# Feed-forward up products with channels as rows: high and low activations move together, wide products before narrow ones

## The chip, the cores and the metric

The kernel runs on one core of one Trainium2 chip. The metric is the device time of one execution, in microseconds (us), the median of several runs.

## What is computed

Two transformer blocks on 256 tokens of width 2048, one after the other, all in float32. The change lies in the last stage, the feed-forward part of the second block. It projects the normalised tokens to 2 x 5632 channels, convolves each channel causally over three tokens, multiplies one half with the silu of the other and projects back:

```
D_MODEL = 2048
FFN_HIDDEN = 5632
CONV_WIDTH = 3
...
def causal_dwconv(u, w, bias):
    ch = u.shape[-1]
    y = lax.conv_general_dilated(u, w[:, None, :].astype(u.dtype), window_strides=(1,),
                                 padding=[(CONV_WIDTH - 1, 0)],
                                 dimension_numbers=('NWC', 'WIO', 'NWC'),
                                 feature_group_count=ch)
    return y + bias
```

In words: `u = rms_norm(x) * (1 + scale) + shift` times `w_up`, `causal_dwconv(u)`, split in two, product with silu, times `w_down`, times a gate, added to `x`.

## The kernel before

**Numbers in two parts.** TensorE works on fp32r operands. To keep float32 accuracy each operand is split into a rounded high part and the low rest. A product is the sum of three: high x high, high x low and low x high. Weights arrive in tiles of two row blocks (`SL = 2`) by 512 channels, 128 x 1024 elements, 512 KB. SyncE loads them into `raw` (8 buffers). ScalarE casts a tile to `hi` (the helper `split`, L728) and VectorE subtracts to get `lo` (L1371), each with 4 buffers (`SPL = 4`); so both run up to four tiles ahead of TensorE and wait for `tile_used`. The activations are already split, in `xh` and `xl`, channel blocks of 128 rows by 256 tokens.

**Token-major products.** `tile` (L2455 to L2457) keeps 128 tokens of the activations in the array and moves 512 weight columns: for each of 2 row blocks and 2 halves of the tokens three products of 512 columns, 12 to a tile. The result has tokens in the rows. Elsewhere in the program `channel_tile` (L2550 to L2552) does it the other way: 128 weight columns stay in the array and 256 tokens move, 24 products of 256 columns to a tile, and the result has channels in the rows.

**The feed-forward stage** goes over `FB = 11` blocks of 512 + 512 channels. For a block, `up_block` takes 16 weight tiles (8 for each half), `down` takes 8 (`c` = 0 to 3, two tiles each). TensorE's order is up(0), up(1), down(0), up(2), down(1) and so on, so that the convolution of a block has a whole up block of time. `half` 0 of the up products is summed in PSUM banks 0 and 1, half 1 in banks 2 and 3, as down uses them in turn as well.

**Between up and down.** ScalarE copies the sum out of PSUM to `UP`, scaled by the root of the norm of each token (`up_evac`, L1274, two instructions of 128x512 to a half). Since the convolution is over tokens, they have to lie along the row: TensorE transposes `UP` to PSUM banks 4 to 7 (`up_turn`, L3132, 8 transposes to a half, 16 to a block). ScalarE then writes the middle tap and the bias to `cv` (`conv_base`, L1283), VectorE adds the other two taps from PSUM (`conv`, L2333, 16 instructions), and silu (L1289), product (L2348), high part `Fh` (L1296) and low part `Fl` (`flow`, L2354) follow. VectorE adds each down result to `Y` (`y_add`, L2377).

**At the stage's head** a row with the norm's square root is put in PSUM bank 7 (`row_of`), VectorE adds shift times that row to the raw activations (`shifted`, L1968 and L1974), ScalarE casts to `xh` (L772, L775), VectorE subtracts to `xl` (`turn_low`). The first up tiles wait for these pair by pair (`turn_lo`).

Of the kernel before, what the change touches and what calls it, by code (L numbers as in the profile page):

```python
# [17 lines left out]
P = 128  # L18
# [3 lines left out]
SL = 2  # L22
# [132 lines left out]
def build(nc, A, out):  # L155
    V, SC, PE_, GP = nc.vector, nc.scalar, nc.tensor, nc.gpsimd
    ctx = ExitStack()
    with ctx:
# [12 lines left out]
        xh = at("xh", [P, KD, S], 64, F32R)  # L171
        xl = at("xl", [P, KD, S], 80, F32R)
# [10 lines left out]
        def C(name, i, n=1):  # L183
# [133 lines left out]
        UP = at("UP", [P, 2, TT, CH], W0 + 32)  # L317
# [79 lines left out]
        up_out, up_T, cv_base, cv_ok, sil_ok, f32_ok, fh_ok, fl_ok, dn_out = (  # L397
            sem(n) for n in ("up_out", "up_T", "cv_base", "cv_ok", "sil_ok", "f32_ok", "fh_ok",
# [136 lines left out]
        def _(pool):  # L535
# [173 lines left out]
            inverse_root(ROOT4, 2, root=True)  # L709
# [8 lines left out]
        def _(act):  # L718
# [49 lines left out]
            def high(n, r):  # L768
                if r == 0:
                    for k in range(2):  # L770
                        act.wait_ge(h_sum, 9 * n + k + 1)
                        SC.copy(xh[:, k], T32[:, k]).then_inc(h_high, 1)  # L772
                    return
# [495 lines left out]
            def up_evac(b, half, n):  # L1269
                act.wait_ge(tile_used, n)  # L1270
                if half == 0 and (not isinstance(b, int) or b):
                    act.wait_ge(up_T, b * 2)
                for t in range(TT):
                    SC.activation(UP[:, half, t], ps[:, 2 * half + t], ACT.Copy,  # L1274
                                  scale=stat[:, ROOT4 + 2 + t:ROOT4 + 3 + t]).then_inc(up_out, 1)

            def conv_base(b, half):

                act.wait_ge(cc_ok, b + 1)
                act.wait_ge(up_T, b * 2 + (half + 1))  # L1280
                for f in range(4):
                    q = 16 * half + 4 * f
                    SC.activation(cv[:, half, f], ps[:, 4 + 2 * half + f // 2, S * (f % 2):S * (f % 2) + S],  # L1283
                                  ACT.Identity, scale=ccol[:, q + 2:q + 3], bias=ccol[:, q + 3:q + 4]
# [71 lines left out]
        def _(dve):  # L1356
# [955 lines left out]
            shifted("h4", 1, 0, 2, ps[:, 7, 0:S])  # L2312
            turn_low(1, 0)
            shifted("h4", 1, 1, 2, ps[:, 7, 0:S])
            shifted("h4", 1, 2, 2, ps[:, 7, 0:S])
            turn_low(1, 1)
            split(BASE["ffn"] + SPL - 1)
            shifted("h4", 1, 3, 2, ps[:, 7, 0:S])
            turn_low(1, 2)

            def conv(b, half):

                for tap in range(2):
# [4 lines left out]
                    for f in range(4):  # L2328
                        q = 16 * half + 4 * f
                        d = 1 + tap  # L2330
                        src = ps[:, 4 + 2 * half + f // 2, S * (f % 2):S * (f % 2) + S - d]
# [39 lines left out]
            def y_add(b, c, n):  # L2371
# [3 lines left out]
                for t in range(TT):  # L2375
                    ys = Y[:, t, c * CH:(c + 1) * CH]
                    V.tensor_tensor(ys, ys, ps[:, 2 * (c % 2) + t], ALU.add).then_inc(dn_out, 1)  # L2377

            def hidden(b, rest):
                conv_cols(b)  # L2380
                rest(2)
                conv(b, 0)
# [5 lines left out]
                flow(b)  # L2388
# [5 lines left out]

            for j in range(2 * TC):
                if j < 4:
                    shifted("h4", 1, 4 + j, 2, ps[:, 7, 0:S])
                split(n0 + SPL + j)
                if j < 5:
                    turn_low(1, 3 + j)  # L2400
            dve.wait_ge(y_zero, 1)
            with dve.Fori(1, FB - 1) as b:
# [4 lines left out]
                hidden(b - 1, rest)  # L2407
                rest(8)
                for c in range(4):
# [4 lines left out]
            hidden(FB - 2, rest)  # L2414
            for c in range(4):
                rest(2)
                y_ready(c)

            conv_cols(FB - 1)
            rest(2)  # L2420
# [17 lines left out]
        def _(pe):  # L2438
# [667 lines left out]
            pe.wait_ge(inv_ok, 2)  # L3106
            row_of(INV, 7)
            keep_busy(9, 6)
            n0 = BASE["ffn"]

            def up_block(b, n, off=0):
                for half in range(2):
                    if not isinstance(b, int):
                        pe.wait_ge(dn_out, b * 8 + (2 * half - 10))
                    elif b:
                        pe.wait_ge(up_out, b * 4 + (2 * half - 2))
                    for j in range(TC):
# [193 lines left out]
```

## Time and profile before

| | |
|---|---|
| median of 3 runs | 3598.34 us (3597.11 to 3598.89) |
| profiled execution, its own time | 3599.18 us |
| span of its profile | 3597.6 us |
| TensorE busy | 3580.8 us |
| VectorE busy | 2667.9 us |
| ScalarE busy | 1782.5 us |
| mean granted TensorE clock | 0.999 of full speed |

The span is the time from the first to the last instruction on the core. An engine's busy time is the sum of the stretches in which it had an instruction under way. A matmul's row in the trace gives a start that can be trusted and an end that is modelled, since products overlap in the array; what a product takes from its neighbours is read from the distance between starts.

### The profile page before, as it was taken

What the parts mean: (1) busy time and instruction counts of PE and PEld (TensorE: products, weight loads), DVE (VectorE), ACT (ScalarE), POOL (GpSimd) and SP (SyncE); (2) the same over time, 40 slices, a digit from 0 to 9 for tenths busy, and PEclk for the clock granted to TensorE, in tenths of its full rate; (3) what the DMA queues carried; (4) which work ended last, traced back from release to release, by engine and by line L of the source; (5) the groups of instructions that cost most, each with busy time, mean ns of one, the idle gap of its engine ahead of it and who ended that gap; (6) DMA issues with size and microseconds to landing.
All of it is one profiled execution on the core that took longest, in us unless ns stands there. A gap on an engine that the chain in (4) does not pass through costs nothing.

```text
span 3597.6 us, 49685 instructions
## 1 busy us (share of the span) xinstructions
PE 3580.8 (100%) x17251; PEld 2993.6 (83%) x17251; DVE 2667.9 (74%) x3480; ACT 1782.5 (50%) x2161; POOL 148.6 (4%) x214
## 2 busy tenths in 40 slices
PE   9999999999999999999999999999999999999999
PEld 7898888888888888888888888878888888888887
DVE  5664567668997877777788887899986656666567
ACT  5554444444444444444444445556754555555444
POOL 4000000000000000000000000010000000000000
PEclk9999999999999999999999999999999999999999
DMA  7546658766668989888887886655556565655654
GB/s 256 170 158 201 193 180 279 270 198 223 206 221 308 356 295 336 298 335 294 339 289 279 279 280 220 184 180 168 168 174 219 174 197 186 192 186 186 192 184 144
DMA packets 211070, 826.96 MB, mean 230 GB/s; under 512 B 24016, under 2 KB 25296, under 8 KB 197088
## 3 DMA queue, kind: packets, MB, share of 16 engines
q1 hardware_dynamic: 177904, 640.23, 53.3%
q10 hardware_dynamic: 15264, 102.99, 7.5%
q0 software_dynamic: 17744, 81.59, 6.2%
q8 instruction: 104, 1.70, 0.2%
q14 instruction: 54, 0.44, 0.0%
HBM read 786.43 MB, written 38.29 MB: 229 GB/s over the span
## 4 chain that ended last, share of the span: by engine, by line
PE 95%; DVE 3%; DMA 1%; issue 1%; ACT 0%; POOL 0%; SPq 0%; ACTq 0%; POOLq 0%; DVEq 0%
PE ps L2455 29%; PE ps L2457 28%; PE ps L2456 28%; PE ps L2811 2%; PE ps L2550 1%; PE ps L2551 1%; PE ps L2552 1%; DVE lo L1371 1%; PE ps L2844 1%; PE ps L2565 1%; PE ps L3132 1%; PE ps L2498 0%; PE ps L2979 0%; DMA act_scratch<-Ab 0%; DVE eq L1773 0%
## 5 line engine op out<-in xcount | busy, mean ns | idle before, releaser
L1371 DVE TENSOR_TENSOR lo<-raw,hi 128x1024 fp32r<-128x1024 f32 x1216 | 1478.4, 1220 | 860.7 <-ACT hi L728 856.9
L728 ACT CAST hi<-raw 128x1024 fp32r<-128x1024 f32 x1216 | 1272.9, 1048 | 1691.4 <-PE ps L2457 1651.2
L2455 PE MATMUL ps<-hi,xh 128*128 128x512 f32 x2880 | 1138.5, 395 | 1.5 <-DVE lo L1371 0.9
L2457 PE MATMUL ps<-hi,xl 128*128 128x512 f32 x2880 | 1123.8, 390 | 0.0
L2456 PE MATMUL ps<-lo,xh 128*128 128x512 f32 x2880 | 1123.2, 390 | 0.0
L2455 PEld LDWEIGHTS ps<-hi,xh 128*128 128x128 f32 x2880 | 541.7, 188 | 117.3 <-issue 6.3
L2457 PEld LDWEIGHTS ps<-hi,xl 128*128 128x128 f32 x2880 | 541.2, 188 | 113.9
L2456 PEld LDWEIGHTS ps<-lo,xh 128*128 128x128 f32 x2880 | 541.9, 188 | 108.7
L2455 PE MATMUL ps<-hi,Ph 128*128 128x512 f32 x1020 | 401.5, 394 | 0.0
L2457 PE MATMUL ps<-hi,Pl 128*128 128x512 f32 x1020 | 397.8, 390 | 0.0
L2456 PE MATMUL ps<-lo,Ph 128*128 128x512 f32 x1020 | 397.3, 390 | 0.0
L2457 PEld LDWEIGHTS ps<-hi,Pl 128*128 128x128 f32 x1020 | 191.5, 188 | 40.2
L2456 PEld LDWEIGHTS ps<-lo,Ph 128*128 128x128 f32 x1020 | 191.8, 188 | 38.5
L2455 PEld LDWEIGHTS ps<-hi,Ph 128*128 128x128 f32 x1020 | 191.6, 188 | 38.5 <-DVE X L1854 0.3
L1854 DVE TENSOR_TENSOR X<-X,ps 128x512 f32<-128x512 f32 x240 | 153.5, 681 | 0.0
L1827 DVE SCALAR_TENSOR_TENSOR macc<-mraw,stat,macc 128x2048 f32<-128x2048 f32 x60 | 140.8, 2346 | 0.2 <-DMA mraw<-in_w_mod 0.2
L2455 PE MATMUL ps<-hi,Fh 128*128 128x512 f32 x348 | 137.7, 396 | 0.7 <-DVE Fl L2354 0.7
L2457 PE MATMUL ps<-hi,Fl 128*128 128x512 f32 x348 | 135.8, 390 | 0.0
L2456 PE MATMUL ps<-lo,Fh 128*128 128x512 f32 x348 | 135.6, 390 | 0.0
L2333 DVE SCALAR_TENSOR_TENSOR cv<-ps,ccol,cv 128x255 f32<-128x255 f32 (+1 forms) x176 | 72.7, 476 | 7.7 <-ACT cv L1283 6.9
L2455 PEld LDWEIGHTS ps<-hi,Fh 128*128 128x128 f32 x348 | 65.4, 188 | 14.4 <-DVE Fl L2354 1.1
L2457 PEld LDWEIGHTS ps<-hi,Fl 128*128 128x128 f32 x348 | 65.3, 188 | 13.8
(478 smaller groups left out, 3574.1 us busy)
## 6 DMA issues: line engine op xcount, KB each, us to landing
raw<-in_peer_u SPq DMA_DIRECT2D x256, 512.0 KB, 4.6
raw<-in_peer_v SPq DMA_DIRECT2D x256, 512.0 KB, 4.6
mraw<-in_w_mod ACTq DMA_DIRECT2D x96, 1024.0 KB, 6.8
raw<-in_w_up SPq DMA_DIRECT2D x176, 512.0 KB, 3.5
raw<-in_w_in SPq DMA_DIRECT2D x143, 512.0 KB, 3.8
raw<-in_in SPq DMA_DIRECT2D x128, 512.0 KB, 3.5
raw<-in_w_down SPq DMA_DIRECT2D x88, 512.0 KB, 4.2
raw<-in_out SPq DMA_DIRECT2D x64, 512.0 KB, 4.2
```

Source lines behind the costliest of these rows:

```text
L728: SC.copy(hi[:, n0 % SPL, 0:w], raw[:, n0 % RAW, 0:w]).then_inc(hi_ready, 1)
L1371: V.tensor_tensor(lo[:, n0 % SPL, 0:w], raw[:, n0 % RAW, 0:w], hi[:, n0 % SPL, 0:w].bitcast(F32), ALU.subtract).then_inc(lo_ready, 1)
L1827: V.scalar_tensor_tensor(macc[:], mraw[:, u % 4], stat[:, 64 + u:65 + u], macc[:], ALU.mult, ALU.add).then_inc(mod_used, 1)
L1854: V.tensor_tensor(xs, xs, ps[:, 4 + 2 * (c % 2) + t], ALU.add).then_inc(v_out, 1)
L2333: ins = V.scalar_tensor_tensor(dst, src, ccol[:, q + 1 - tap:q + 2 - tap], dst, ALU.mult, ALU.add)
L2455: PE_.matmul(acc, xhi[:, k0 + k, xs], H, start=s0, stop=False)
L2456: PE_.matmul(acc, xhi[:, k0 + k, xs], L, start=False, stop=False)
L2457: mm = PE_.matmul(acc, xlo[:, k0 + k, xs], H, start=False, stop=s1)
L2550: PE_.matmul(acc, H, xhi[:, k0 + k], start=first and k == 0 and f % 2 == 0, stop=False)
L2551: PE_.matmul(acc, H, xlo[:, k0 + k], start=False, stop=False)
L2552: mm = PE_.matmul(acc, L, xhi[:, k0 + k], start=False, stop=last and k == SL - 1 and f % 2 == 1)
L2811: mm = PE_.matmul(ps[:, 4 + b, k * P:(k + 1) * P], oh1[:, b, k], oh2[:, b, k], start=True, stop=True)
```

## The change

Up products are made with channels in the rows. The high and low activations become one tensor `xx`, and the high weights meet both in one product whose moving operand is 2 x 256 columns, the high tokens and behind them the low ones; it fills a whole PSUM bank (columns 0 to 255 high x high, 256 to 511 high x low). The low weights meet the high tokens in a product of 256 columns, added to columns 0 to 255. In `up_tile` all 8 wide products of a tile come first and then its 8 narrow ones. An up half takes 4 banks, so the two halves and the four down results each use all 8. ScalarE copies the first half of each bank to `UP` (one instruction), VectorE adds the second half (`up_sum`, new), and the convolution reads `UP`. The transposes are gone, and so is the scaling on the way out: the root is multiplied into the activations ahead of their split (`rooted`, `rooted_low`), and ScalarE adds the shift as it casts.

```
--- before.py
+++ after.py
...
-        xh = at("xh", [P, KD, S], 64, F32R)
-        xl = at("xl", [P, KD, S], 80, F32R)
+        xx = at("xx", [P, 2, KD, S], 64, F32R)
+        xh, xl = xx[:, 0], xx[:, 1]
...
-        UP = at("UP", [P, 2, TT, CH], W0 + 32)
+        UP = at("UP", [P, 2, 4, S], W0 + 32)
...
-            inverse_root(ROOT4, 2, root=True)
+            inverse_root(ROOT4, 2)
...
+                if n == 1:
+                    for k in range(2):
+                        act.wait_ge(h_sum, 9 + (k + 1 if r == 0 else r + 2))
+                        SC.activation(xh[:, 2 * r + k], T32[:, 2 * r + k], ACT.Identity,
+                                      bias=mcol[:, 2, 2 * r + k:2 * r + k + 1]).then_inc(h_high, 1)
+                    return
...
             def up_evac(b, half, n):
                 act.wait_ge(tile_used, n)
-                if half == 0 and (not isinstance(b, int) or b):
-                    act.wait_ge(up_T, b * 2)
-                for t in range(TT):
-                    SC.activation(UP[:, half, t], ps[:, 2 * half + t], ACT.Copy,
-                                  scale=stat[:, ROOT4 + 2 + t:ROOT4 + 3 + t]).then_inc(up_out, 1)
+                if not isinstance(b, int) or b:
+                    act.wait_ge(cv_ok, b * 2 + (half - 1))
+                SC.copy(UP[:, half], ps[:, 4 * half:4 * half + 4, 0:S]).then_inc(up_high, 1)
 
             def conv_base(b, half):
 
                 act.wait_ge(cc_ok, b + 1)
-                act.wait_ge(up_T, b * 2 + (half + 1))
+                act.wait_ge(up_out, b * 2 + (half + 1))
                 for f in range(4):
                     q = 16 * half + 4 * f
-                    SC.activation(cv[:, half, f], ps[:, 4 + 2 * half + f // 2, S * (f % 2):S * (f % 2) + S],
-                                  ACT.Identity, scale=ccol[:, q + 2:q + 3], bias=ccol[:, q + 3:q + 4]
+                    SC.activation(cv[:, half, f], UP[:, half, f], ACT.Identity, scale=ccol[:, q + 2:q + 3], bias=ccol[:, q + 3:q + 4]
                                   ).then_inc(cv_base, 1)
 
...
+            def rooted(r):
+                dve.wait_ge(turn_hi, 2 * (TBASE["h4"] + r) + 2)
+                if r == 0:
+                    for k in range(2):
+                        V.tensor_tensor(T32[:, k], T32[:, k], row4, ALU.mult).then_inc(h_sum, 1)
+                    return
+                both = T32[:, 2 * r:2 * r + 2]
+                V.tensor_tensor(both, both, row4.unsqueeze(1).to_broadcast([P, 2, S]), ALU.mult).then_inc(h_sum, 1)
+
+            def rooted_low(r):
+                for k in range(2):
+                    c = 2 * r + k
+                    dve.wait_ge(h_high, 9 + c + 1)
+                    dve.wait_ge(h_sum, 9 + (k + 1 if r == 0 else r + 2))
+                    low = V.scalar_tensor_tensor(xl[:, c], T32[:, c], mcol[:, 2, c:c + 1], xh[:, c].bitcast(F32),
+                                                 ALU.add, ALU.subtract)
+                    if k:
+                        low.then_inc(turn_lo, 1)
+                    elif r == 0:
+                        low.then_inc(pair_low, 1)
+
+            rooted(0)
+            rooted_low(0)
+            rooted(1)
+            rooted(2)
+            rooted_low(1)
             split(BASE["ffn"] + SPL - 1)
-            shifted("h4", 1, 3, 2, ps[:, 7, 0:S])
-            turn_low(1, 2)
+            rooted(3)
+            rooted_low(2)
 
...
-                        src = ps[:, 4 + 2 * half + f // 2, S * (f % 2):S * (f % 2) + S - d]
+                        src = UP[:, half, f, 0:S - d]
...
+                dve.wait_ge(up_out, b * 2 + 2)
...
-                flow(b)
...
+            def up_sum(b, half, n):
+                dve.wait_ge(tile_used, n)
+                dve.wait_ge(up_high, b * 2 + (half + 1))
+                V.tensor_tensor(UP[:, half], ps[:, 4 * half:4 * half + 4, S:2 * S], UP[:, half], ALU.add).then_inc(up_out, 1)
+
...
                 hidden(b - 1, rest)
+                up_sum(b, 0, off + (n0 + 24))
+                flow(b - 1)
                 rest(8)
+                up_sum(b, 1, off + (n0 + 32))
...
-            pe.wait_ge(inv_ok, 2)
-            row_of(INV, 7)
+            pe.wait_ge(rstd_ready, ROOTS)
+            row_of(ROOT4 + 2, 7)
             keep_busy(9, 6)
             n0 = BASE["ffn"]
+
+            def up_tile(n0, off, k0, bank, first, last, ready=None):
+
+                pe.wait_ge(lo_ready, n0 + 1 + FIRST + off)
+                for k in range(SL):
+                    if ready is not None:
+                        ready(k)
+                    for f in range(4):
+                        H = hi[:, n0 % SPL, k * CH + f * P:k * CH + (f + 1) * P]
+                        both = ps[:, bank + f].rearrange("p (a t) -> p a t", a=2)
+                        PE_.matmul(both, H, xx[:, :, k0 + k], start=first and k == 0, stop=False)
+                for k in range(SL):
+                    for f in range(4):
+                        L = lo[:, n0 % SPL, k * CH + f * P:k * CH + (f + 1) * P]
+                        mm = PE_.matmul(ps[:, bank + f, 0:S], L, xh[:, k0 + k], start=False, stop=last and k == SL - 1)
+                mm.then_inc(tile_used, 1)
 
             def up_block(b, n, off=0):
                 for half in range(2):
                     if not isinstance(b, int):
-                        pe.wait_ge(dn_out, b * 8 + (2 * half - 10))
+                        pe.wait_ge(dn_out, b * 8 + (4 * half - 12))
                     elif b:
-                        pe.wait_ge(up_out, b * 4 + (2 * half - 2))
+                        pe.wait_ge(up_out, half + 1)
                     for j in range(TC):
                         first = isinstance(b, int) and b + half == 0
                         if first and j:
                             pe.wait_ge(turn_lo, TBASE["h4"] + j + 1)
-                        tile(n + TC * half + j, off, xh, xl, SL * j, 2 * half, j == 0, j == TC - 1,
-                             ready=h4_pair if first and j == 0 else None)
-                        if isinstance(b, int) and b < 2 and b + half == 1 and j == 2:
-                            up_turn(0, b)
-
-            def up_turn(b, half):
-                pe.wait_ge(up_out, b * 4 + (2 * half + 2))
-                if not isinstance(b, int) or b:
-                    pe.wait_ge(cv_ok, b * 2 + (half - 1))
-                for f in range(4):
-                    for t in range(TT):
-                        mm = PE_.transpose(ps[:, 4 + 2 * half + f // 2, (f % 2) * S + t * P:(f % 2) * S + (t + 1) * P],
-                                           UP[:, half, t, f * P:(f + 1) * P], ident)
-                mm.then_inc(up_T, 1)
+                        up_tile(n + TC * half + j, off, SL * j, 4 * half, j == 0, j == TC - 1,
+                                ready=h4_pair if first and j == 0 else None)
 
             def down(b, c, n, off=0):
 
@@ -3139,23 +3183,17 @@
...
                     pe.wait_ge(fl_ok, b + 1)
-                elif c >= 2 and sum_open:
-                    pe.wait_ge(cv_ok, 2 * (FB - 1) + c - 1)
-                elif c >= 2 and not last:
-                    pe.wait_ge(dn_out, b * 8 + (2 * c - 2))
-                bank = 2 * c if sum_open or last else 2 * (c % 2)
+                if c % 2 == 0 and not last:
+                    pe.wait_ge(up_out, b * 2 + (3 + c // 2))
...
+            def downs(b, n, off=0):
+
+                for c in range(4):
                     down(b, c, n, off)
```

On TensorE at the head of the loop over blocks, where the down products of block b - 2 begin (`up_out`, `cv_ok`, `fl_ok` are semaphores counted by ScalarE and VectorE, `ISA` and `REGISTER_ALU` rows are waits and the counting of them), before:

```order
L3129 ISA [waits up_out]
L3132 MATMUL ps<-const,UP 128x128 [waits cv_ok]
L3132 MATMUL ps<-const,UP 128x128 x7
L2442 ISA [waits fl_ok]
L2455 MATMUL ps<-hi,Fh 128x512 [waits lo_ready]
```

and after, with the first up tile of the same loop under it:

```order
L3187 ISA [waits fl_ok]
L2482 ISA [waits up_out]
L2495 MATMUL ps<-hi,Fh 128x512 [waits lo_ready]
...
L3153 REGISTER_ALU [waits dn_out]
L3160 MATMUL ps<-xx,hi 128x512 [waits lo_ready]
L3160 MATMUL ps<-xx,hi 128x512 x7
L3164 MATMUL ps<-xx,lo 128x256 x8
```

The transposes have gone from the front of the down products, which now wait for VectorE's sum (`up_out`); an up tile is 8 wide and 8 narrow products where it was 12 wide ones.

On VectorE, behind the product of the convolved halves in the same loop, before:

```order
L2348 TENSOR_TENSOR F32t<-cv,sil 128x1024 [waits cv_ok]
L1369 REGISTER_ALU
L1371 TENSOR_TENSOR lo<-raw,hi 128x1024 [waits hi_ready]
L1369 REGISTER_ALU
L1371 TENSOR_TENSOR lo<-raw,hi 128x1024 [waits hi_ready]
L2354 TENSOR_TENSOR Fl<-F32t,Fh 128x1024 [waits f32_ok,fh_ok]
```

and after:

```order
L2374 TENSOR_TENSOR F32t<-cv,sil 128x1024 [waits cv_ok,sil_ok]
L1372 REGISTER_ALU
L1374 TENSOR_TENSOR lo<-raw,hi 128x1024 [waits hi_ready]
L1372 REGISTER_ALU
L1374 TENSOR_TENSOR lo<-raw,hi 128x1024 [waits hi_ready]
L2423 ISA [waits tile_used]
L2424 TENSOR_TENSOR UP<-ps,UP 128x1024 [waits up_high]
L2380 TENSOR_TENSOR Fl<-F32t,Fh 128x1024 [waits f32_ok,fh_ok]
```

The new sum stands ahead of `Fl`, so `Fl` and the weight splits behind it come after a wait for the last product of an up half (`tile_used`) and for ScalarE's copy (`up_high`). The second sum of a block stands eight splits later.

## Rows read from the trace of the kernel before

**Rows 1.** The page: busy times, the granted clock, the chain by engine.
```profile
PE 3580.8 (100%) x17251; PEld 2993.6 (83%) x17251; DVE 2667.9 (74%) x3480; ACT 1782.5 (50%) x2161; POOL 148.6 (4%) x214
...
PEclk9999999999999999999999999999999999999999
...
PE 95%; DVE 3%; DMA 1%; issue 1%; ACT 0%; POOL 0%; SPq 0%; ACTq 0%; POOLq 0%; DVEq 0%
```

**Rows 2.** Windows: one feed-forward block each; engines' busy us (instructions), clock, DMA.
```profile
3144.20:3211.30 67.10, 67.10 (x306) 55.74 (x305) 42.63 (x51) 35.26 (x41) 0.00 (x0) 1.00 0.58 187
3211.30:3278.40 67.10, 67.10 (x306) 55.74 (x305) 42.62 (x51) 35.25 (x41) 0.00 (x0) 1.00 0.57 188
```

**Rows 3.** Chain that ended last, 3130 to 3290 us: start, us, what.
```profile
3144.16 0.87 PE ps L3132 x8
3150.50 0.87 PE ps L3132 x8
...
3211.26 0.87 PE ps L3132 x8
```

**Rows 4.** Timeline of TensorE, up tiles (24 products between the first and the last row).
```profile
3204.97 0.39 PE L2455 MATMUL ps<-hi,xh 128*128 128x512 f32 x1
3205.20 0.39 PE L2456 MATMUL ps<-lo,xh 128*128 128x512 f32 x1
...
3210.41 0.39 PE L2455 MATMUL ps<-hi,xh 128*128 128x512 f32 x1
```

**Rows 5.** Timeline of TensorE in channel_tile (42 products between first and last row).
```profile
2285.04 0.28 PE L2550 MATMUL ps<-xh,hi 128*128 128x256 f32 x1
2285.16 0.28 PE L2551 MATMUL ps<-xl,hi 128*128 128x256 f32 x1
...
2290.08 0.28 PE L2550 MATMUL ps<-xh,hi 128*128 128x256 f32 x1
```

**Rows 6.** One line's instructions, channel_tile's low weights: ns min/median/max, first and last start.
```profile
L2552 PEld LDWEIGHTS ps<-yh,lo x64: 188/192/193, 2675.6 to 2698.5; 128*128 128x128 f32 x64
```

**Rows 7.** Groups by form, 2900 us to the end: busy us, mean ns, idle before.
```profile
L1371 DVE TENSOR_TENSOR lo<-raw,hi 128x1024 fp32r<-128x1024 f32 x245 | 298.9, 1224 | 229.3 <-ACT hi L728 229.1
L728 ACT CAST hi<-raw 128x1024 fp32r<-128x1024 f32 x244 | 255.8, 1052 | 294.5 <-PE ps L2457 294.4
L2377 DVE TENSOR_TENSOR Y<-Y,ps 128x512 f32<-128x512 f32 x72 | 46.1, 681 | 0.0
L2333 DVE SCALAR_TENSOR_TENSOR cv<-ps,ccol,cv 128x255 f32<-128x255 f32 x88 | 36.4, 476 | 6.9 <-ACT cv L1283 6.9
L1274 ACT ACTIVATE UP<-ps,stat 128x512 f32<-128x512 f32 x42 | 26.4, 679 | 0.0
```

**Rows 8.** Timeline of TensorE, last down(FB-2): two gaps.
```profile
3559.07 0.39 PE L2457 MATMUL ps<-hi,Fl 128*128 128x512 f32 x1
3559.49 0.50 PE L2455 MATMUL ps<-hi,Fh 128*128 128x512 f32 x1
...
3570.32 0.39 PE L2457 MATMUL ps<-hi,Fl 128*128 128x512 f32 x1
3571.40 0.50 PE L2455 MATMUL ps<-hi,Fh 128*128 128x512 f32 x1 [0.69 <-DVE Fl L2354]
```

**Rows 9.** Timelines ahead of the second gap: VectorE's convolution, then ScalarE.
```profile
3556.10 3.34 DVE L2333 SCALAR_TENSOR_TENSOR cv<-ps,ccol,cv 128x255 f32<-128x255 f32 x8 [0.60 <-ACT cv L1283]
3559.74 3.34 DVE L2333 SCALAR_TENSOR_TENSOR cv<-ps,ccol,cv 128x255 f32<-128x255 f32 x8 [0.30 <-ACT cv L1283]
...
3568.08 1.05 ACT L728 CAST hi<-raw 128x1024 fp32r<-128x1024 f32 x1 [1.67 <-PE ps L2457]
3569.04 1.04 ACT L1296 CAST Fh<-F32t 128x1024 fp32r<-128x1024 f32 x1
```

**Rows 10.** Timelines at the stage's head: GpSimd, TensorE's first product, VectorE's rounds.
```profile
2849.68 1.63 POOL L552 TENSOR_TENSOR stat<-stat,half 128x2 f32<-128x2 f32 x1 [137.69 <-DVE stat L2306]
2851.30 0.68 POOL L553 TENSOR_TENSOR stat<-stat,neghalf 128x2 f32<-128x2 f32 x1
...
2853.64 0.47 PE L2455 MATMUL ps<-hi,xh 128*128 128x512 f32 x1 [0.58 <-DVE xl L1981]
...
2857.46 0.48 DVE L1968 SCALAR_TENSOR_TENSOR T<-ps,mcol,T 128x256 f32<-128x256 f32 x1
2857.85 0.48 DVE L1974 SCALAR_TENSOR_TENSOR T<-ps,mcol,T 128x256 f32<-128x256 f32 x1
2858.24 0.68 DVE L1988 TENSOR_TENSOR xl<-T,xh 128x512 fp32r<-128x512 f32 x1
2858.84 0.48 DVE L1968 SCALAR_TENSOR_TENSOR T<-ps,mcol,T 128x256 f32<-128x256 f32 x1
```

More of the change, by code:

```diff
@@ L396, in build @@
         br_out = sem("br_out")
-        up_out, up_T, cv_base, cv_ok, sil_ok, f32_ok, fh_ok, fl_ok, dn_out = (
-            sem(n) for n in ("up_out", "up_T", "cv_base", "cv_ok", "sil_ok", "f32_ok", "fh_ok",
+        up_out, up_high, cv_base, cv_ok, sil_ok, f32_ok, fh_ok, fl_ok, dn_out = (
+            sem(n) for n in ("up_out", "up_high", "cv_base", "cv_ok", "sil_ok", "f32_ok", "fh_ok",
                              "fl_ok", "dn_out"))
@@ L2311, in _ @@
             dve.wait_ge(inv_ps, 3)
[L2312 to L2316, printed above, removed]
+            row4 = ps[:, 7, 0:S]
+            def rooted(r):
[22 more added lines that the diff above has]
+            rooted_low(1)
             split(BASE["ffn"] + SPL - 1)
-            shifted("h4", 1, 3, 2, ps[:, 7, 0:S])
-            turn_low(1, 2)
+            rooted(3)
+            rooted_low(2)
             def conv(b, half):
@@ L2376, in y_add @@
                     ys = Y[:, t, c * CH:(c + 1) * CH]
-                    V.tensor_tensor(ys, ys, ps[:, 2 * (c % 2) + t], ALU.add).then_inc(dn_out, 1)
+                    V.tensor_tensor(ys, ys, ps[:, 2 * c + t], ALU.add).then_inc(dn_out, 1)
             def hidden(b, rest):
@@ L2393, in rest @@
                     local[0] += 1
+            def up_sum(b, half, n):
+                dve.wait_ge(tile_used, n)
+                dve.wait_ge(up_high, b * 2 + (half + 1))
+                V.tensor_tensor(UP[:, half], ps[:, 4 * half:4 * half + 4, S:2 * S], UP[:, half], ALU.add).then_inc(up_out, 1)
             for j in range(2 * TC):
                 if j < 4:
-                    shifted("h4", 1, 4 + j, 2, ps[:, 7, 0:S])
+                    rooted(4 + j)
                 split(n0 + SPL + j)
                 if j < 5:
-                    turn_low(1, 3 + j)
+                    rooted_low(3 + j)
+                if j % TC == TC - 1:
+                    up_sum(0, j // TC, n0 + j + 1)
             dve.wait_ge(y_zero, 1)
@@ L2414, in _ @@
             hidden(FB - 2, rest)
+            up_sum(FB - 1, 0, TOTAL - 24)
+            flow(FB - 2)
             for c in range(4):
@@ L2417, in _ @@
                 y_ready(c)
+            up_sum(FB - 1, 1, TOTAL - 16)
             conv_cols(FB - 1)
+            dve.wait_ge(up_out, 2 * FB)
             rest(2)
@@ L3141, in down @@
                     pe.wait_ge(fl_ok, b + 1)
-                elif c >= 2 and sum_open:
-                    pe.wait_ge(cv_ok, 2 * (FB - 1) + c - 1)
-                elif c >= 2 and not last:
-                    pe.wait_ge(dn_out, b * 8 + (2 * c - 2))
-                bank = 2 * c if sum_open or last else 2 * (c % 2)
+                if c % 2 == 0 and not last:
+                    pe.wait_ge(up_out, b * 2 + (3 + c // 2))
                 for j in range(TL):
                     if n + TL * c + j == TOTAL - 1:
-                        last_tile(TOTAL - 1, h, l, SL * j, bank)
+                        last_tile(TOTAL - 1, h, l, SL * j, 2 * c)
                     else:
-                        tile(n + TL * c + j, off, h, l, SL * j, bank, j == 0 and not last, j == TL - 1 and not sum_open)
-            def down_and_turn(b, n, off=0):
-                up_turn(b + 1, 0)
-                down(b, 0, n, off)
-                up_turn(b + 1, 1)
-                for c in range(1, 4):
+                        tile(n + TL * c + j, off, h, l, SL * j, 2 * c, j == 0 and not last, j == TL - 1 and not sum_open)
+            def downs(b, n, off=0):
+                for c in range(4):
                     down(b, c, n, off)
@@ L3165, in _ @@
             with pe.Fori(2, FB) as b:
-                down_and_turn(b - 2, n0 + 32, b * 24 - 48)
+                downs(b - 2, n0 + 32, b * 24 - 48)
                 up_block(b, n0 + 40, b * 24 - 48)
-            down_and_turn(FB - 2, n0 + 24 * FB - 16)
-            for c in range(4):
-                down(FB - 1, c, n0 + 24 * FB - 8)
+            downs(FB - 2, n0 + 24 * FB - 16)
+            downs(FB - 1, n0 + 24 * FB - 8)
 def constants():
```

## Prediction

> **What bounds the kernel now.** I read the page first: TensorE is busy in all of the span and makes up 95% of the chain that ended last, at the full granted clock of 2.4 GHz in every slice [rows 1]. So the question is what each product and each transpose takes of TensorE's time, and whether another engine would make it wait. The windows of two feed-forward blocks answer the second: each takes 67.10 us, in which TensorE has no idle time, VectorE is busy for 42.6 and ScalarE for 35.3 [rows 2]. The groups say what those two wait for: VectorE for ScalarE's cast, and ScalarE for TensorE to free a weight buffer (294 us of idle time in this stage [rows 7]). They are ahead of TensorE by as much as the four buffers let them. The reader should see that only TensorE's own work counts here, unless a new wait breaks the lead.
>
> **The price of a product.** Starts tell it, not lengths. In the up tiles 24 products of 512 columns lie between 3204.97 and 3210.41 us: 5.44 / 24 = 0.2267 us each [rows 4]. At 2.4 GHz, 512 columns are 0.2133, so a product carries 13.3 ns beside its columns. In channel_tile 42 products of 256 columns lie between 2285.04 and 2290.08: 5.04 / 42 = 0.1200 us each [rows 5], of which columns are 0.1067: 13.3 ns again. The charge goes by product, not by column. A tile before costs 12 x 0.2267 = 2.720 us.
>
> **Up tiles after.** 8 wide and 8 narrow ones move the same 6144 columns, in 16 products for 12: 8 x 0.2267 + 8 x 0.1200 = 2.773 us, 0.053 more. There are 16 x 11 = 176 up tiles: +9.4 us. This takes the wide product, whose moving operand is in two runs of 256 columns, at the price of one in one run. No row shows such a product. Its bounds: the 0.2133 us of its bare columns below, and the price of two narrow products, 0.2400, above. I take 0.2267, because it is one instruction with one weight load and 512 columns, as the nearest row is. The narrow ones come eight in a row with other weights each; in channel_tile two of three share weights, yet a load stands before each product there as well, and the distance is 0.12 after either kind. So 0.12 is taken, with 0.1067 as the lower bound and the load's own row, 0.192 [rows 6], as the upper; the loads in channel_tile last 0.192 each by their rows and yet come every 0.12, so they overlap and the upper bound is remote.
>
> **Page and row on the charge.** The Trainium skill, "TensorE: Matmul & The Clock Gate", section "Back-to-back issue gap", gives the columns at 2.4 GHz plus about 2.5 ns. By that an up tile would go from 12 x 215.8 = 2.590 us to 8 x (215.8 + 109.2) = 2.600, and the added cost would be 1.8 us in all. The trace disagrees with it, with 13.3 ns at both widths, and the trace decides.
>
> **Transposes removed.** A block's period is 3211.26 - 3144.16 = 67.10 us [rows 3]. Its 24 tiles are 24 x 2.720 = 65.28. What is left, 1.82 us, is the two groups of 8 transposes with the slower start of the products behind them, 0.91 for a group. There are 22 groups in the stage: -20.0 us. TensorE waits for nothing in a block, so this is work taken off, not a wait moved.
>
> **Waits.** TensorE now waits for VectorE's sum of an up half before down products write its banks. For half 0 this is eight tiles after the half's end. For half 1 it is four tiles, since down's first two parts use banks 0 to 3: 4 x 2.72 = 10.9 us. What has to fit: a cast already due (1.05), the copy of 128x1024 by ScalarE (1.05 as the cast of that size), a split on VectorE (1.22) and the sum (1.22 as the split of that size; y_add's 0.68 for half as many elements from PSUM agrees) [rows 7]: 4.5 us at the worst, one behind the other. The up products wait for two y_adds where it was three, with four tiles in hand where it was two. Queued behind the new sum on VectorE are Fl, needed eight tiles later, and the next split, which has three tiles (8 us) in hand. VectorE gets 2 x 1.22 us more to a block: 45.1 of 66. ScalarE loses four instructions of 0.68 and gets two of about 1.05. All of this I cost at nothing, and what hides it is the lead of three tiles; if it failed, each us of stall in a block would be 10 to 11 us in the time.
>
> **Head.** GpSimd's first instruction (square root, 1.63 us) was awaited, the second not (0.68) [rows 10]. Now one is left and awaited. It gains between nothing and 0.95 us; I take nothing, since it is the first after a long idle time, as the 1.63 was. VectorE's chain to the first product keeps its length: two multiplications and two subtractions of the same sizes. A round on VectorE was two instructions of 0.39 us by their starts, one of 0.60 [rows 10] and a split; it is now one of 0.60, two of 0.39 and a split. Zero, plus or minus 0.5.
>
> **Tail.** In the last down(FB-2) there were two gaps. The first, 0.42 us between starts for 0.23, came from the convolution still reading PSUM; it goes: -0.2, with a slow first product -0.3. The second, 1.08 for 0.23, comes from Fl, behind Fh, behind a cast that waits for the seventh of the eight tiles [rows 8, 9]. That order stays, and so does the gap. With the transposes gone TensorE reaches the sixth tile's end about as VectorE, after the 16 convolution instructions, 8 in 3.3 us [rows 9], gets to that split: +0.2. Together nothing.
>
> **The sum.** +9.4 - 20.0 = -10.6 us. The block should go from 67.10 to 16 x 2.773 + 8 x 2.720 = 66.13. The profiled execution took 3599.18 us (span 3597.6), so 3588.6; the median is 0.8 lower than it, 3598.34 - 10.6 = 3587.7. A difference below 0.2% (7.2 us) can't be told from none in this kernel.
>
> **The rivals.**
> A, the sum as above: 3587.7 us, 3586 to 3589.5 with head and tail. Chance 0.73.
> B, slower: the wide product pays for its two runs. At the price of two narrow ones each of the 176 x 8 = 1408 costs 13.3 ns more, +18.8: 3606.5 us. It eats the gain from 7.5 ns (18 cycles) on. For it: no row shows such an operand. Against: the 13.3 ns goes with an instruction and its weight load, and there is one of each. Chance 0.07. The Trainium skill, "PSUM — Partial Sum Buffer", section "Specifications (TRN2)", says that non-contiguous patterns slow matmuls significantly; here the pattern in PSUM is a whole bank and only the moving one has a gap, so no run here shows yet whether it speaks to this case.
> C, slower: the narrow products are bound by their weight loads, since no two share weights now. At 0.192 us for 0.12 it would be 1408 x 0.072 = +101: 3689 us. Against it, the even 0.12 in [rows 5]. Chance 0.02.
> D, a lead is lost: the sum or the copy comes late once in a block, or ScalarE's copy delays a cast, and TensorE stalls for up to 1 us a block. It gives back up to the whole gain: 3589 to 3598, about 3594 us. For it: VectorE has the longest queue in the last half of a block. Against: no idle time in 67 us now, and slack above 6 us. Chance 0.12.
> E, more is won: the 13.3 ns comes partly from three products in a row into one bank, which the new order avoids. Without it an up tile is 2.56 us, -0.16 x 176 = -28 in place of +9.4: 3550 us. Against: before, every third product changes bank and the distances stay even at 0.23 [rows 4]. A page's 2.5 ns would be of this kind too. Chance 0.06.
>
> **How the numbers follow.** The time is A's. Faster by over 0.2% means below 3591.1: A but for a little, E, and a piece of D: 0.79. Within 0.2%: most of D, a trace of A and a B of less than 12 ns: 0.13. Slower: the rest of B, and C: 0.08. The range leaves out B, C and E (0.15) and takes in nearly all of D: 3583 to 3597. A's own range is 3586 to 3589.5.
>
> **What would show it.** In the profile after, the transposes are gone, starts of wide products stand 0.227 apart and narrow ones 0.120, a block repeats every 66.1 us, and TensorE has no idle time in it; VectorE's busy time in a block is about 45 us. Wide starts at 0.235 or more say B, narrow ones above 0.125 C, idle time before the down or up products (released by the sum or y_add) D, distances under 0.22 and 0.115 E. The gap before the first product with Fh of the last block stays near 1 us.

## The result and the profile after

The changed kernel takes 3591.64 us (median of 20 runs, 3590.51 to 3594.41), the kernel before 3598.23 us (20 runs, 3597.11 to 3600.4): 6.6 us less, a ratio of 0.9982 with a 95% interval from 0.9976 to 0.9988. The forecast was 10.6 us less. The time lies in the range that was given, and just above the 3591.1 us below which "faster by over 0.2%" began.

The page after, its busy times, granted clock and chain, beside those of [rows 1]:

```profile
PE 3572.4 (100%) x17779; PEld 3010.2 (84%) x17779; DVE 2692.1 (75%) x3502; ACT 1783.8 (50%) x2146; POOL 147.9 (4%) x213
...
PEclk9999999999999999999999999999999999999999
...
PE 94%; DVE 3%; DMA 1%; issue 1%; ACT 0%; POOL 0%; SPq 0%; ACTq 0%; DVEq 0%; POOLq 0%
```

TensorE is busy for 8.4 us less with 528 more products, still at full clock, and still the chain. The windows of two stretches of 66.50 us in the feed-forward stage (busy us of TensorE, its weight loads, VectorE, ScalarE, GpSimd; clock, DMA), which answer to [rows 2]:

```profile
3137.00:3203.50 66.50, 66.50 (x354) 57.40 (x353) 44.94 (x53) 35.30 (x39) 0.00 (x0) 1.00 0.62 190
3203.50:3270.00 66.50, 66.50 (x354) 57.41 (x353) 44.94 (x53) 35.30 (x39) 0.00 (x0) 1.00 0.62 189
```

TensorE has no idle time, and VectorE's 44.9 us is what was worked out (45.1). So no wait ate the missing 4 us. TensorE's timeline after, the start of an up block, its end with the down products that follow, and the next up block (a row is one product or several of one kind, as x8 says; its first number is the start, and a run cut by the edge of the stretch that was asked for shows only a part of its products):

```profile
3164.08 1.98 PE L3160 MATMUL ps<-xx,hi 128*128 128x512 f32 x8
3165.90 1.12 PE L3164 MATMUL ps<-xx,lo 128*128 128x256 f32 x8
3166.85 1.32 PE L3160 MATMUL ps<-xx,hi 128*128 128x512 f32 x5
3167.78 0.62 PE L3160 MATMUL ps<-xx,hi 128*128 128x512 f32 x2
...
3169.64 2.00 PE L3160 MATMUL ps<-xx,hi 128*128 128x512 f32 x8
3171.48 1.11 PE L3164 MATMUL ps<-xx,lo 128*128 128x256 f32 x8
3172.43 2.00 PE L3160 MATMUL ps<-xx,hi 128*128 128x512 f32 x8
...
3208.75 0.40 PE L2495 MATMUL ps<-hi,Fh 128*128 128x512 f32 x1
...
3230.53 0.62 PE L3160 MATMUL ps<-xx,hi 128*128 128x512 f32 x2
```

Read it by starts. A block repeats after 3230.53 - 3164.08 = 66.45 us, where 66.13 was forecast and 67.10 measured before. Its down part is 21.78, for the 8 x 2.720 = 21.76 of the forecast; its up part is 44.67 for 44.37. A tile is 3172.43 - 3169.64 = 2.79 us for 2.773. The eight wide products take 1.84 us in a tile that follows narrow ones, and 1.82 in the first tile of the block, which follows the 512-column products of the down part. Over all tiles of the stage the wide run behind narrow products takes 28 ns more than 8 x 0.2267, and the narrow run behind wide ones 8 ns less than 8 x 0.1200. So 20 ns a tile went missing, and they are lost just behind a narrow run. The experiments ask what they are.

### The profile page after: what moved, and what is told of

It is laid out like the page before. It is cut to its first block, busy times and chain, and to the rows that moved or that the text cites. A ratio compares the mean times of both kernels' runs of the same rounds, so it can differ in the third digit from the quotient of the medians.

```text
span 3590.2 us, 50766 instructions
## 1 busy us (share of the span) xinstructions
PE 3572.4 (100%) x17779; PEld 3010.2 (84%) x17779; DVE 2692.1 (75%) x3502; ACT 1783.8 (50%) x2146; POOL 147.9 (4%) x213
## 4 chain that ended last, share of the span: by engine, by line
PE 94%; DVE 3%; DMA 1%; issue 1%; ACT 0%; POOL 0%; SPq 0%; ACTq 0%; DVEq 0%; POOLq 0%
PE ps L2495 24%; PE ps L2497 24%; PE ps L2496 24%; PE ps L3160 9%; PE ps L3164 5%; PE ps L2851 2%; PE ps L2590 1%; PE ps L2591 1%; PE ps L2592 1%; DVE lo L1374 1%; PE ps L2884 1%; PE ps L2605 1%; PE ps L2538 0%; DMA gate_scratch<-gst 0%; PE ps L3019 0%
## 5 line engine op out<-in xcount | busy, mean ns | idle before, releaser
L2495 PE MATMUL ps<-hi,xx 128*128 128x512 f32 x2176 | 862.7, 396 | 1.0 <-DVE lo L1374 0.9
L2497 PE MATMUL ps<-hi,xx 128*128 128x512 f32 x2176 | 848.5, 390 | 0.0
L2496 PE MATMUL ps<-lo,xx 128*128 128x512 f32 x2176 | 847.8, 390 | 0.0
L2495 PEld LDWEIGHTS ps<-hi,xx 128*128 128x128 f32 x2176 | 409.2, 188 | 88.8 <-issue 5.5
L2497 PEld LDWEIGHTS ps<-hi,xx 128*128 128x128 f32 x2176 | 408.7, 188 | 86.4
L2496 PEld LDWEIGHTS ps<-lo,xx 128*128 128x128 f32 x2176 | 409.3, 188 | 81.5
L3160 PE MATMUL ps<-xx,hi 128*128 128x512 f32 x1408 | 352.6, 392 | 0.7 <-DVE xx L2331 0.7
L3160 PEld LDWEIGHTS ps<-xx,hi 128*128 128x128 f32 x1408 | 253.8, 189 | 46.7 <-issue 0.9
L3164 PEld LDWEIGHTS ps<-xx,lo 128*128 128x128 f32 x1408 | 192.1, 190 | 13.7
L3164 PE MATMUL ps<-xx,lo 128*128 128x256 f32 x1408 | 196.4, 282 | 0.0
```

The costliest lines, as they stand in the source:

```text
L2495: PE_.matmul(acc, xhi[:, k0 + k, xs], H, start=s0, stop=False)
L2496: PE_.matmul(acc, xhi[:, k0 + k, xs], L, start=False, stop=False)
L2497: mm = PE_.matmul(acc, xlo[:, k0 + k, xs], H, start=False, stop=s1)
L3160: PE_.matmul(both, H, xx[:, :, k0 + k], start=first and k == 0, stop=False)
L3164: mm = PE_.matmul(ps[:, bank + f, 0:S], L, xh[:, k0 + k], start=False, stop=last and k == SL - 1)
```

## Experiments

**The order of the products in a tile.** Four kernels make the same products of the changed kernel and differ in order or layout alone. `wide(k, f)` and `narrow(k, f, stop)` are helpers that make one wide and one narrow product as `up_tile` did. The first alternates:

```diff
                     for f in range(4):
-                        H = hi[:, n0 % SPL, k * CH + f * P:k * CH + (f + 1) * P]
-                        both = ps[:, bank + f].rearrange("p (a t) -> p a t", a=2)
-                        PE_.matmul(both, H, xx[:, :, k0 + k], start=first and k == 0, stop=False)
-                for k in range(SL):
-                    for f in range(4):
...
+                        wide(k, f)
+                        mm = narrow(k, f, last and k == SL - 1)
```

> An up tile of the changed kernel takes 2.793 us where 2.773 was forecast: 8 wide products 1.84 where 1.813 was forecast, 8 narrow ones 0.95. This run makes the same 16 products of a tile in another order, each wide one followed by its narrow one. Theory T1, the 20 ns are paid at each return from narrow to wide products: 8 returns for 1, so 2.773 + 8 x 0.020 = 2.93 us a tile, a feed-forward block of 16 x 2.93 + 8 x 2.72 = 68.7 us, 25 us above the changed kernel. Theory T1b, they are paid by the length of the run of narrow products before: the sum stays, block 66.45 us, time 3591.6. Theory T2, a wide product costs 2.5 ns more because its moving operand is in two runs: order is nothing, block 66.45 us. Theory T3, the wait at a tile's head costs it: block 66.45 us.

The second has runs of four:

```diff
...
-                for k in range(SL):
+                        wide(k, f)
                     for f in range(4):
...
+                        mm = narrow(k, f, last and k == SL - 1)
```

> The same products, 4 wide and 4 narrow for the first row block of a tile, then 4 and 4 for the second: two returns from narrow to wide in a tile for one. T1 (each return costs 20 ns): 2.813 us a tile, block 66.77 us, about 3.5 us above the changed kernel. T1b (by length of the narrow run), T2 (two runs of the moving operand), T3 (wait at the head): block 66.45 us, no difference.

In the third, narrow runs of two neighbouring tiles meet:

```diff
+                order = [(wide, k, f) for k in range(SL) for f in range(4)]
+                narrows = [(narrow, k, f) for k in range(SL) for f in range(4)]
+                order = narrows + order if (k0 // SL) % 2 else order + narrows
```

> The same products, but every second tile makes its narrow ones first, so that narrow runs of two tiles meet (16 in a row) and wide ones too: one return in two tiles. T1: 2.783 us a tile, block 66.29 us, 1.8 us under the changed kernel (3589.9). T1b: a longer narrow run costs as much as two, block 66.45. T2, T3: block 66.45 us.

The fourth keeps the order and puts the operand of a wide product in one run:

```diff
-        xx = at("xx", [P, 2, KD, S], 64, F32R)
+        T4 = at("T4", [P, KD, S], W0 + 32)
+        xx4 = at("xx4", [P, KD, 2, S], 64, F32R)
...
-                        PE_.matmul(both, H, xx[:, :, k0 + k], start=first and k == 0, stop=False)
+                        PE_.matmul(both, H, xx4[:, k0 + k], start=first and k == 0, stop=False)
```

> High and low activations of a row block lie next to each other, so the wide product's moving operand is one run of 512 columns; the raw activations are kept in another place for that, all else is as in the changed kernel. T2 (two runs cost 2.5 ns a product): wide products 0.2267 apart from the first on, tile 2.773 us, block 66.13 us, 3.5 us under the changed kernel (3588.1). T1, T1b, T3: no difference, block 66.45 us, 8 wide products still 1.84 us.

What they took, an up block read from the first up product's start to the first down product's, as above; by the prices of single products it would be 44.37 us. The down part behind it, 96 products of 512 columns, would be 21.76 us:

| kernel | narrow run | wide run behind it | returns in an up block | up block, us | over 44.37 | per return | down part, us | median, us |
|---|---|---|---|---|---|---|---|---|
| alternating | 1 | 1 | 127 | 45.21 | 0.84 | 7 ns | 21.82 | 3597.69 |
| by row block | 4 | 4 | 31 | 44.88 | 0.51 | 16 ns | 21.80 | 3594.10 |
| changed kernel | 8 | 8 | 15 | 44.67 | 0.30 | 20 ns | 21.79 | 3591.64 |
| back to back | 16 | 16 | 8 | 44.53 | 0.16 | 20 ns | 21.76 | 3589.88 |
| one run | 8 | 8 | 15 | 44.67 | 0.30 | 20 ns | 21.79 | 3591.49 |

The two ends of that reading for the kernel with runs of four, TensorE's timeline:

```profile
3165.81 0.62 PE L3156 MATMUL ps<-xx,hi 128*128 128x512 f32 x2
...
3210.69 0.40 PE L2495 MATMUL ps<-hi,Fh 128*128 128x512 f32 x1
```

and for the one with tiles back to back:

```profile
3162.49 0.84 PE L3156 MATMUL ps<-xx,hi 128*128 128x512 f32 x3
...
3207.02 0.39 PE L2495 MATMUL ps<-hi,Fh 128*128 128x512 f32 x1
```

One theory falls at once: with its operand in one run a wide product costs what it did, to the hundredth of a us in a block (T2). The wait at a tile's head (T3) falls as well, since the order changes the time and the number of waits does not. The returns remain. T1, 20 ns at each return, holds for runs of 8 and 16 and about for 4 (expected 3.5 us above the changed kernel, measured 2.5), and is wrong for single ones, where it asked for 25 us more and 6 came. T1b, a price by length of the run, is wrong for all of them.

The starts say where a return is paid. It is spread over the first five wide products, 28 ns in all over 5 x 0.2267, and it is the same behind 8 and behind 16 narrow products; 8 ns come back in the first two narrow products of a run. In the two kernels with a smaller price per return the wide runs are shorter too. TensorE's timeline with runs of four:

```profile
3186.83 1.09 PE L3156 MATMUL ps<-xx,hi 128*128 128x512 f32 x4
3187.76 0.63 PE L3160 MATMUL ps<-xx,lo 128*128 128x256 f32 x4
```

and alternating:

```profile
3209.64 0.40 PE L3156 MATMUL ps<-xx,hi 128*128 128x512 f32 x1
3209.88 0.28 PE L3160 MATMUL ps<-xx,lo 128*128 128x256 f32 x1
```

Four wide products behind four narrow ones take 0.93 us, where 0.907 are due, and the first four behind eight narrow ones in the changed kernel take the same 0.93 (3167.78 - 3166.85). A wide product that stands alone takes 0.24. What such short wide runs don't pay shows up later: the down part is 21.82 and 21.80 us behind these two up blocks, 21.79 behind that of the changed kernel and 21.76 behind the one that ends with wide products. So the 7 and 16 ns don't show that a short narrow run costs less. The lengths of both runs were changed together and no run here separates them; the starts speak for the wide one.

**Price by product.** In the next kernel each wide product is made as two narrow ones:

```diff
+                        for a, x in enumerate((xh, xl)):
+                            PE_.matmul(ps[:, bank + f, a * S:(a + 1) * S], H, x[:, k0 + k],
+                                       start=first and k == 0 and a == 0, stop=False)
```

> Each wide product of the changed kernel is made as two narrow ones (high weights with high tokens, then the same weights with low tokens), 24 products of 256 columns to a tile, all else as in the changed kernel. If a product carries 13.3 ns whatever its width, a tile is 24 x 0.1200 = 2.880 us, an up block 46.08 us (44.67 in the changed kernel) and a feed-forward block 67.86 us, with the 0.02 us of one return to 512 columns: time 3591.6 + 11 x 1.41 = 3607.2 us, slower than before. If instead weight loads or something else binds long narrow runs, more; if the charge belongs to the change of weights and not to the product, the two products that share weights cost 0.227 together and the block stays at 66.4.

3606.42 us, ratio 1.0022 (1.0012 to 1.0031). The up block on TensorE's timeline, and the first down products after 384 narrow ones:

```profile
3171.47 0.76 PE L3169 MATMUL ps<-xx,hi 128*128 128x256 f32 x5
...
3217.54 0.40 PE L2495 MATMUL ps<-hi,Fh 128*128 128x512 f32 x1
3217.78 0.40 PE L2496 MATMUL ps<-lo,Fh 128*128 128x512 f32 x1
3218.01 0.39 PE L2497 MATMUL ps<-hi,Fl 128*128 128x512 f32 x1
3218.24 0.40 PE L2495 MATMUL ps<-hi,Fh 128*128 128x512 f32 x1
3218.47 0.39 PE L2496 MATMUL ps<-lo,Fh 128*128 128x512 f32 x1
3218.70 0.39 PE L2497 MATMUL ps<-hi,Fl 128*128 128x512 f32 x1
```

The up block is 46.07 us, and 384 x 0.1200 = 46.08: the charge of 13.3 ns goes by product, also where two in a row have the same weights. Moving high and low together saves 1.4 us a block against this kernel: 128 charges of 13.3 ns, less 0.3 us for the returns. The rows behind it show the return from near: distances of 0.24, 0.23, 0.23, 0.23, 0.23, where a long wide run has 0.2267; 1.16 us for the first five, where 1.133 are due. After 384 narrow products it is the same 28 ns as after 8.

**A floor under a product.** Each narrow product as two of 128 columns:

```diff
+                        for t in range(TT):
+                            tok = slice(t * P, (t + 1) * P)
+                            mm = PE_.matmul(ps[:, bank + f, tok], L, xh[:, k0 + k, tok], start=False,
+                                            stop=last and k == SL - 1 and t == 1)
```

> Each narrow product of the changed kernel is made as two of 128 columns (the same low weights, first and second half of the tokens): 24 products to a tile, 6144 columns. If the charge of 13.3 ns goes on by product, one of 128 columns takes 0.0667 us, a narrow run 16 x 0.0667 = 1.07 us for 0.96, a tile 2.90, the block 66.45 + 16 x 0.107 = 68.2 us. If 0.12 us is a floor under any product with its weight load, which the narrow ones have reached, the run takes 16 x 0.12 = 1.92 us and the block goes to 81.8 us. In between: a floor between 0.067 and 0.12, which the start distances then give.

3741.38 us, ratio 1.0399 (1.0383 to 1.0415). TensorE's timeline in an up block:

```profile
3201.05 1.90 PE L3166 MATMUL ps<-xx,lo 128*128 128x128 f32 x16
3202.78 2.07 PE L3160 MATMUL ps<-xx,hi 128*128 128x512 f32 x8
3204.69 1.90 PE L3166 MATMUL ps<-xx,lo 128*128 128x128 f32 x16
```

The block is 80.0 us, between the 68.2 and the 81.8 of the expectation. The loads of the 16 products, and the next ones:

```profile
3200.82 1.98 PEld L3166 LDWEIGHTS ps<-xx,lo 128*128 128x128 f32 x16
3202.72 0.30 PEld L3160 LDWEIGHTS ps<-xx,hi 128*128 128x128 f32 x2
```

16 loads from 3200.82 to 3202.72 are 0.119 apart with the entry, and the products' run of 1.73 us is 0.108 each, with a first one of 0.06; past the entry both stand 0.112 apart. It is some 0.11 us, not the 0.067 of columns and charge. So there is a floor of about 0.11 us under a product with a load of its own, and the 256-column product with 0.12 stands just above it. It fits the returns: the wide run behind these 16 takes 3204.69 - 3202.78 = 1.91 us, 0.10 over its 1.813, over three times the 28 ns behind a narrow run that stays above the floor. The Trainium skill, "TensorE: Matmul & The Clock Gate", section "LDWEIGHTS (loading the stationary operand)", gives a load its columns / 1.2 in ns; worked out from it, 128 columns are an estimated 107 ns, and the measured 0.108 to 0.119 us lie close to it. The load rows themselves last 0.19 us each, and overlap. That a return is the time in which loads win back their place ahead of the products is what these numbers suggest; no run here took the loads apart from the products, so this stays argued.

**The transposes by themselves.** Put back into the changed kernel, of the identity, with their result overwritten:

```diff
+                if c < 2 and not last:
+                    for _ in range(8):
+                        PE_.transpose(ps[:, 2 * c, 0:P], ident, ident)
```

> The changed kernel with 8 transposes of the identity put ahead of the first and of the second down product of each block but the last one's (20 groups in all, their result is overwritten). It prices the term of what was removed by itself: 0.91 us a group, block 66.45 + 1.82 = 68.27 us, time 3591.6 + 20 x 0.91 = 3609.8 us. If the groups had cost less by themselves and part of the 0.91 was something else of the old order, less: half of it would give a block of 67.4 us.

3608.78 us, ratio 1.0031 (1.002 to 1.0043). TensorE's timeline, a block apart:

```profile
3146.06 1.04 PE L3190 MATMUL ps<-const 128*128 128x128 f32 x8
...
3214.28 1.04 PE L3190 MATMUL ps<-const 128*128 128x128 f32 x8
```

The block is 68.22 us, 1.77 more than 66.45: 0.885 us a group, for 0.91 expected. The first group of a block stands where the changed kernel pays a return, so some 28 ns of it are hidden in this difference: by itself a group costs about 0.90.

**The cover of VectorE's sum.** Each sum made four times:

```diff
+                for i in range(3):
+                    V.tensor_tensor(more[:, i], ps[:, 4 * half:4 * half + 4, S:2 * S], UP[:, half], ALU.add)
                 V.tensor_tensor(UP[:, half], ps[:, 4 * half:4 * half + 4, S:2 * S], UP[:, half], ALU.add).then_inc(up_out, 1)
```

> The changed kernel with each of VectorE's 22 sums of an up half made four times, three of them into spare memory: 6 x 1.15 = 6.9 us more of VectorE's time in a block (44.9 becomes 51.8 of 66.5) and the real sum 3.4 us later. The theory that the lead of the weight splits covers all work of this kind expects no change: block 66.45 us, time 3591.6. The rival that part of the lead was used up by the new sum expects idle time of TensorE in the block and 1 us or more a block, 3603 us and above.

3596.92 us, 5.3 above the changed kernel. A window in the loop, then TensorE's waits from 2840 us to the end (us in total, times, longest):

```profile
3166.00:3233.00 67.00, 67.00 (x359) 57.89 (x358) 51.84 (x61) 35.51 (x39) 0.00 (x0) 1.00 0.60 191
```

```profile
PE ps L2498 <- DVE lo L1375: 3.7, 2, 3.0
PE ps L2876 <- POOL stat L554: 1.0, 1, 1.0
PE ps L3163 <- DVE xx L2332: 0.7, 1, 0.7
PE ps L2498 <- DVE Fl L2381: 0.5, 1, 0.5
PE ps L2944 <- DVE X L2304: 0.3, 1, 0.3
```

In the loop the cover held: no idle time with VectorE at 51.8 us, and the block still 66.45. The rival with 1 us a block is out. But the expectation of no change at all failed, in one place: in the last block the sum is followed by 16 convolution instructions and only then by the next split, and TensorE waited 3.0 us for `lo`. VectorE's timeline there:

```profile
3546.29 3.49 DVE L2426 TENSOR_TENSOR more<-ps,UP 128x1024 f32<-128x1024 f32 x3
3549.69 1.22 DVE L2427 TENSOR_TENSOR UP<-ps,UP 128x1024 f32<-128x1024 f32 x1
...
3553.30 6.65 DVE L2360 SCALAR_TENSOR_TENSOR cv<-UP,ccol,cv 128x255 f32<-128x255 f32 x16
3559.87 2.35 DVE L1375 TENSOR_TENSOR lo<-raw,hi 128x1024 fp32r<-128x1024 f32 x2
```

The waits don't make up the 5.3 us. TensorE's timeline behind the long one, then a window of it:

```profile
3561.14 0.50 PE L2498 MATMUL ps<-hi,Fh 128*128 128x512 f32 x1 [3.02 <-DVE lo L1375]
...
3562.86 0.63 PE L2498 MATMUL ps<-hi,Fh 128*128 128x512 f32 x1
3563.28 0.63 PE L2499 MATMUL ps<-lo,Fh 128*128 128x512 f32 x1
```

```profile
3562.43:3565.82 3.39, 3.39 (x10) 2.67 (x9) 3.20 (x3) 0.11 (x1) 0.00 (x0) 0.51 0.79 290
```

From 1.3 us after the 3.0 us of idle time the granted clock was 0.51 for 3.4 us, the level of 1.2 GHz, and eight products stood 0.42 apart in place of 0.2267: 1.6 us. With 3.2 and 0.8 us at the two waits for `lo` that is 5.6 us, of which the changed kernel loses 0.4 at its own gaps there: 5.2 of the 5.3. From the stage's first up product to the down products behind the last up block both kernels take 687.8 us, so all of it falls behind them.

**The best order, side by side.** The kernel with tiles back to back once more, and the changed kernel on the same chip:

> The order with narrow runs of two tiles back to back, once more and beside the changed kernel on the same chip: 8 returns in an up block for 16. By the blocks (66.29 us for 66.45) it should be 1.8 us under the changed kernel, 3589.9 for 3591.6; if the difference seen before was between chips or calls, none.

> The changed kernel as it is, beside the one above: 3591.6 us, block 66.45 us.

Back to back 3589.93 us, ratio 0.9977 (0.9967 to 0.9986); the changed kernel 3591.78 us, ratio 0.9982 (0.9973 to 0.9991). The difference is the 1.8 us of the expectation, here and between the first two runs, and the blocks show where it is (66.29 us for 66.45). The intervals of the ratios overlap; the case for it rests on the blocks.

## Why the prediction came out as it did

The sum forecast 10.6 us and 6.6 came, so the measured time is 2.1 us above the upper end of A's own range, 3589.5. The wider range holds it only because it left room for rival D, a wait, and no wait came: that the time fell into it is luck. Of the outcomes, "faster by over 0.2%" had a chance of 0.79 and "within 0.2%", where the median lies, had 0.13; the interval of the ratio holds both.

- **What bounds the kernel**: right. TensorE's own work counts, before and after, at full clock.
- **Transposes removed, -20.0 us**: right within 0.5. 22 x 0.885 = 19.5 us, by the transposes put back; 22 x 0.90 = 19.8 with the return that they hide.
- **Up tiles, +9.4 us**: the step that was mis-sized. The prices of single products held (0.120 narrow, 0.2267 wide, 13.3 ns by product), but "8 x 0.2267 + 8 x 0.1200 = 2.773" adds the prices of two even rhythms and leaves out the change from one to the other. It costs 20 ns at each return, 15 in an up block, and 28 ns at the one into its down part: an up block is 44.67 us for the 43.52 of before, +1.15 x 11 = +12.6 us. The reader could have seen it in the trace of before, where channel_tile hands over to the 512-column products. Its timeline there:

```profile
2290.32 0.28 PE L2552 MATMUL ps<-xh,lo 128*128 128x256 f32 x1
2290.44 0.40 PE L2455 MATMUL ps<-hi,xh 128*128 128x512 f32 x1
2290.68 0.40 PE L2456 MATMUL ps<-lo,xh 128*128 128x512 f32 x1
2290.91 0.39 PE L2457 MATMUL ps<-hi,xl 128*128 128x512 f32 x1
```

  0.24 and 0.23 for 0.2267: I read both rhythms from their middles and never looked at the seam.
- **The page's price for a product**: the formula that the prediction took from the Trainium skill, "TensorE: Matmul & The Clock Gate", section "Back-to-back issue gap", is given there for a product by itself, and for a stream of loads and products the section has 81 ns at 128 columns and 131 ns at 512. The traces here have about 111 and 226.7 ns, so neither describes these products.
- **The bounds of the wide product**: the choice of 0.2267 in two runs was right; rival B is out by the kernel with one run, and rival E by the starts: wide products that go to one bank after another settle at 0.2267.
- **Rival C**, weight loads as the bound of the narrow run: out at 256 columns, but nearer than the 0.192 us of the load's own row made it look. The floor of some 0.11 us is 8% below.
- **Waits at nothing**: right in the loop, with 6.9 us of VectorE's time to spare at least. Rival D did not come. In the tail it was a near thing, as the +0.2 said. TensorE's timeline after, the answer to [rows 8]:

```profile
3557.14 0.39 PE L2497 MATMUL ps<-hi,Fl 128*128 128x512 f32 x1
3557.64 0.50 PE L2495 MATMUL ps<-hi,Fh 128*128 128x512 f32 x1
...
3563.00 0.39 PE L2497 MATMUL ps<-hi,Fl 128*128 128x512 f32 x1
3564.07 0.50 PE L2495 MATMUL ps<-hi,Fh 128*128 128x512 f32 x1 [0.69 <-DVE Fl L2380]
```

  The first gap is now the split's lateness in place of the convolution's (0.50 us between starts for 0.42), the second is as it was (1.07 for 1.08).
- **Head**: at nothing, right. GpSimd's one instruction takes the same time as the first of two did, and from its start to the first up product are 4.06 us for the 3.96 of before [rows 10]:

```profile
2849.19 1.63 POOL L553 TENSOR_TENSOR stat<-stat,neghalf 128x2 f32<-128x2 f32 x1 [137.69 <-DVE stat L2309]
...
2853.25 0.70 PE L3160 MATMUL ps<-xx,hi 128*128 128x512 f32 x2 [0.68 <-DVE xx L2331]
```

The sum with the measured terms is -19.5 + 12.6 = -6.9 us; block by block it is 11 x (66.45 - 67.10) = -7.2; measured -6.6, with an interval of the ratio that reaches from -8.6 to -4.3.

## What to carry to other kernels

Count products and not columns when operands are paired or split: each with its load cost 13.3 ns beside its columns here, and below some 0.11 us it got no cheaper. Where rhythms of two widths meet, look at the seam, not at the middles: going back from narrow to wide cost 20 ns where both runs were of eight or more, so gather the narrow ones across tiles. Slack has to be asked for place by place: the loop hid 7 us of added work in each block for nothing, and the last block charged 5.3 us for it, of which 1.6 us came from the lower clock behind a wait of 3 us.

## What the runs showed of the hardware

- A moving operand of 512 columns in two runs, 16 KB apart, costs what one run costs (up block 44.67 us either way).
- Behind 8, 16 or 384 products of 256 columns the first five of 512 columns took 28 ns more in all than five even ones, and the first two narrow products behind wide ones 8 ns less. With wide runs of four and of one the net price per return was 16 and 7 ns, and more was left for the products of 512 columns behind them (down part 21.80 and 21.82 us for 21.79). Behind products of 128 columns a wide run of eight took 0.10 us more.
- Behind 3.0 us without work TensorE ran 1.3 us at the granted clock of 0.97 and then 3.4 us at 0.51, with products of 512 columns 0.42 us apart.
- A product with its own weight load takes about 0.11 us at 128 columns, nearly the 0.120 of 256.
- GpSimd's first power of two numbers took 1.63 us with either exponent, the one behind it 0.68 [rows 10].
